# The token of the dot products kept in PSUM instead of SBUF, in a two-layer decoder step with expert retrieval

## The reference, cut to what matters

```
q = (xb @ w_q)                                  # queries, per head 2 halves of 128
s = einsum('bhcd,hcnd->bhcn', q, sk)            # scores against 2 x 128 keys
sv, si = lax.top_k(s, 16) ...                   # two top-16, their 256 sums, top-16 of these
hpre = einsum('bd,bhkd->bhk', xb, u_tab[eid])   # dot products of the token with 128 rows of u
a = gelu(hpre) * softmax(fv)
out = einsum('bhk,bhkd->bd', a, v_tab[eid])     # weighted sum of 128 rows of v
```

## Time and profile before

| | us |
|---|---|
| median of three runs (4362.62, 4367.6, 4372.01) | 4367.6 |
| span of the profiled execution, first to last instruction | 4356.4 |
| POOL busy | 2601.7 |
| DVE busy | 2837.7 |
| PE busy | 2784.1 |
| ACT busy | 601.9 |

### The profile page before, as it was taken

How to read it: one execution, slowest core, us unless ns; L and a number is a source line. 1 busy time by engine, 2 the same in 40 slices (tenths; PEclk the granted TensorE clock), 3 DMA queues, 4 the chain that set the end, 5 groups by cost and what they waited for, 6 DMA issues and landing times.

```text
span 4356.4 us, 41077 instructions
## 1 busy us (share of the span) xinstructions
PE 2784.1 (64%) x7573; PEld 1355.0 (31%) x7573; DVE 2837.7 (65%) x6064; ACT 601.9 (14%) x1614; POOL 2601.7 (60%) x2313
## 2 busy tenths in 40 slices
PE   1498366666656656766778863666666566666566
PEld 1354223233322323322344442232232223322222
DVE  7902777777767777766334347767777677677754
ACT  2110111111111111111122111111111111111011
POOL 2000277777777777776600014778777677777774
PEclk9699688888878888888999976888888888888899
DMA  1540399999999999999900134999999899999997
GB/s 44 44 194 26 121 362 372 370 357 370 379 334 354 374 347 351 368 382 409 398 1 0 52 127 159 364 360 352 356 362 373 328 362 368 342 353 365 359 402 299
DMA packets 355457, 1267.52 MB, mean 291 GB/s; under 512 B 39292, under 2 KB 52092, under 8 KB 351868
## 3 DMA queue, kind: packets, MB, share of 16 engines
q0 software_dynamic: 331776, 1208.11, 73.9%
q1 hardware_dynamic: 23508, 57.71, 4.7%
HBM read 1261.31 MB, written 4.82 MB: 291 GB/s over the span
## 4 chain that ended last, share of the span: by engine, by line
PE 33%; DVE 19%; issue 19%; DMA 14%; POOL 9%; ACT 3%; DVEq 1%; SPq 1%; POOLq 0%; ACTq 0%
PE ps L1370 20%; DMA arena<-in_peer_v,idxv 7%; DMA arena<-in_peer_u,idxu 5%; POOL arena L1577 5%; POOL arena L1565 4%; PE ps L1318 3%; DVE arena L723 2%; DVE arena L712 2%; DVE arena L424 2%; PE ps L1444 2%; PE ps L1459 2%; ACT arena L1064 1%; DVE arena L657 1%; DVE picked L660 1%; PE ps L1340 1%
## 5 line engine op out<-in xcount | busy, mean ns | idle before, releaser
L1370 PE MATMUL ps<-arena 128*128 128x512 f32 x3584 | 1900.8, 679 | 1175.1 <-ACT arena L1064 811.4
L1565 POOL DMA_INDIRECT arena<-in_peer_u,idxu x1152 | 1261.1, 1095 | 1141.8 <-issue 736.0
L712 DVE CUSTOM_DVE_ANT_0 arena<-arena 128x1024 bf16<-128x1024 f32 x1152 | 1387.8, 1226 | 630.6 <-DMA arena<-in_peer_u,idxu 545.7
L1577 POOL DMA_INDIRECT arena<-in_peer_v,idxv x1152 | 1304.7, 1133 | 451.8 <-issue 312.5
L1370 PEld LDWEIGHTS ps<-arena 128*128 128x128 f32 x3584 | 733.4, 216 | 2239.7 <-issue 2114.3
L1064 ACT ACTIVATE arena<-ident,av 128x128 f32<-128x128 f32 x768 | 259.5, 394 | 673.4 <-DVE av L706 423.4
L723 DVE SCALAR_TENSOR_TENSOR arena<-arena,av 128x1024 f32 (+1 forms) x256 | 328.4, 1283 | 6.7 <-DMA arena<-in_peer_v,idxv 6.3
L1340 PE MATMUL ps<-arena 128*128 (+1 forms) x1280 | 300.2, 389 | 10.0 <-DMA arena<-in_peer_wq 5.2
L1340 PEld LDWEIGHTS ps<-arena 128*128 128x128 f32 x1280 | 248.2, 196 | 69.9 <-issue 29.3
L622 DVE MAX8 top<-arena 128x8 f32<-128x128 f32 x128 | 37.0, 289 | 175.0 <-ACT arena L1043 174.7
L1318 PE MATMUL ps<-arena 128*128 128x512 f32 (+1 forms) x320 | 139.7, 599 | 4.4 <-DMA arena<-in_w_glu 4.4
(11 more groups left out here) (214 smaller groups left out, 1966.2 us busy)
## 6 DMA issues: line engine op xcount, KB each, us to landing
arena<-in_peer_u,idxu POOLq DMA_INDIRECT x1152, 6.3
arena<-in_peer_v,idxv POOLq DMA_INDIRECT x1152, 6.3
arena<-in_peer_wq SPq DMA_DIRECT2D x4, 4096.0 KB, 19.8
arena<-in_w_glu SPq DMA_DIRECT2D x2, 4096.0 KB, 13.3
arena<-kern SPq DMA_DIRECT2D x8, 512.0 KB, 22.0
arena<-in_w_q SPq DMA_DIRECT2D x1, 4096.0 KB, 22.9
arena<-in_w_o SPq DMA_DIRECT2D x1, 4096.0 KB, 41.8
arena<-in_gains SPq DMA_DIRECT2D x6, 512.0 KB, 17.5
```

The lines of the kernel that those rows point to most:

```text
L712: dve.tensor_tensor_reduce(JUNK[:, k % 2, :], UROWS[:, k % NU_RING, :], XCUR, 1.0, 0.0, ALU.mult, ALU.add, hp[:, par, k:k + 1]).then_inc(S ...
L1370: mm = pe.matmul(ps[:, half, :], DIAG[:, i % 4, :], VROWS[k % NV_RING][:, half * 512:(half + 1) * 512], start=(starts and i == 0), stop=Fa ...
L1565: pool.indirect_dma_start(UROWS[:, k % NU_RING, :], None, tab_u, bass.IndirectOffsetOnAxis(ap=idxu[:, par, k:k + 1], axis=0))\
L1577: pool.indirect_dma_start(VROWS[k % NV_RING], None, tab_v, bass.IndirectOffsetOnAxis(ap=idxv[:, par, k:k + 1], axis=0))\
```

## The change

The area `XCUR` in SBUF goes; the token is kept in banks 6 and 7 of PSUM. The copy at a tile's first head writes there, and all 16 dots of a slot read it from there. For this, the queries of both parities share bank 4 (columns 0 to 255 and 256 to 511), and the turned queries and the scores of both parities share bank 5: for each parity, the scores are written over the turned queries of the same head.

```diff
-        XCUR = area(20480, D)
...
+        XCUR = ps[:, 6:8, :].rearrange("p a b -> p (a b)")
+        QP = ps[:, 4, :].rearrange("p (a n) -> p a n", a=2)
+        QTP = ps[:, 5, :].rearrange("p (a n) -> p a n", a=2)
...
-                    act.copy(QN[:, par, :], ps[:, 4 + par, 0:2 * P]).then_inc(S["q_copied"], 1)
+                    act.copy(QN[:, par, :], QP[:, par, :]).then_inc(S["q_copied"], 1)
...
-                    act.copy(QT[:, par].rearrange("p a n -> p (a n)"), ps[:, 6 + par, 0:2 * P]).then_inc(S["qt_copied"], 1)
+                    act.copy(QT[:, par].rearrange("p a n -> p (a n)"), QTP[:, par, :]).then_inc(S["qt_copied"], 1)
...
-                    act.copy(SC[:, par].rearrange("p a n -> p (a n)"), ps[:, 6 + par, 256:512]).then_inc(S["sc_copied"], 1)
+                    act.copy(SC[:, par].rearrange("p a n -> p (a n)"), QTP[:, par, :]).then_inc(S["sc_copied"], 1)
...
-                        mm = pe.matmul(ps[:, 4 + par, 0:2 * P], XT[:, k, :],
+                        mm = pe.matmul(QP[:, par, :], XT[:, k, :],
...
-                        mm = pe.transpose(ps[:, 6 + par, i * P:(i + 1) * P], QN[:, par, i * P:(i + 1) * P], ident[:, :])
+                        mm = pe.transpose(QTP[:, par, i * P:(i + 1) * P], QN[:, par, i * P:(i + 1) * P], ident[:, :])
...
-                        mm = pe.matmul(ps[:, 6 + par, 256 + i * P:256 + (i + 1) * P], QT[:, par, i, :],
+                        mm = pe.matmul(QTP[:, par, i * P:(i + 1) * P], QT[:, par, i, :],
```

## The result

The changed kernel takes 4291.35 us (median of 4 runs, 4289.13 to 4293.61), the kernel before 4367.06 in runs beside it: a ratio of 0.9826, with a 95% interval of 0.9812 to 0.984, so 76 us less. The forecast was 4129, 238 us less, with 4055 to 4250. The direction was right, the size was three times too large, and the time lies 41 us above the range.

A forecast was written before the change was run, and what follows sets the result against it. The prediction took POOL to set the pace, its gathers held by DVE's dots. From 4367.6 us, 270 us of released gathers less 16, 10 and 5 left 239 us less: 4129 us, range 4055 to 4250.

The forecast's parts named there:

- That two inputs in SBUF hold a gather and one in PSUM does not: POOL's gathers beside DVE's dots: of 404.6 us above the median gather length (the excess), 270 us goes.
- the short operations: DVE's two 0.69 us operations at and after line 657, 64 times in the slots: they still hold gathers, 17 us.
- The dot's own duration: 1152 dots on DVE: reading the token from PSUM costs 0 us more each.
- the copy of the token into PSUM: DVE's token copy, 10 times: 1.22 us instead of 0.694, so 5 us of the gain is lost.
- The shared banks: PE's queries, turned queries and scores in banks 4 and 5: no added wait in 80 heads, 0 us.
- the rival in which DVE gets slower: The custom dot reads its inputs in turn and takes 2.3 us: at least +236, 4604 us; chance 0.04.
- the one in which the dot still holds POOL: The custom dot holds gathers whatever its inputs are: no gain, 4368 + 5 us; chance 0.05.
- POOL sets the pace before: Both retrievals, 3459 us: POOL's gathers 2565.8, issue 691 and about 200 us of waits set the rows' pace.
- What is late next: Per slot after the change: POOL needs 41.6 us, DVE (33.3 busy) and PE (29.5) stay below that.
- The terms for what doesn't shorten the span: Gain lost at layer starts (16 us), at first heads (10 us) and to the token copy (5 us).
- DMA: Rival in the retrievals: DMA is the bound, ending at 360 GB/s (4368 us) or 380 (4207); chance 0.08.
- The rival with DVE and the rings taking half of the gain: DVE's back-to-back work sets the slot and, with the rings of 8 rows, takes half: 4248 us; chance 0.05.

The follow-up runs named there:

- both moves: Weights made ahead of a slot's first two dots, searches and merge later in DVE's program: 4430.2 us on the kernel before, 4186.8 us on the changed kernel.
- the later searches: Changed kernel with the two top-16 searches and the merge two, two and one dots later in DVE's program: 4179.7 us.
- the versions at 4180: Changed kernel with searches and merge later (4179.7 us), with weights sooner as well (4186.8), or the latter with the merge one dot sooner (4179.1).
- early weights: Kernel before, with the last slot's weights made ahead of the first two dots instead of behind them: 4400.5 us.

## Why the prediction was wrong, point by point

- **That two inputs in SBUF hold a gather and one in PSUM does not: right**, on a custom instruction too. Some 750 gathers inside dots, none held. Of the excess 276 us went, where 270 were forecast, and 129 stayed, where 135 were. That this came so near is in part luck, as two terms missed to opposite sides: 99 us lie on gathers that start inside row adds (115 forecast, 0.39 us for each row add in place of 0.45) and 31 us on those that start inside the short operations (17 forecast).
- **The dot's own duration: right** (1.218 us, forecast 1.22), and so the copy of the token into PSUM (1.228 us, forecast 1.22). **The shared banks: right**, 0 us, by their own run. With them the rival in which DVE gets slower is out, and so is the one in which the dot still holds POOL.
- **POOL sets the pace before: right as far as it went**: with both moves on the kernel before, its excess grew by 97 us and the span by 84, though the wait for the scores had gone. But it set the pace by a narrow margin, as the next point shows.
- **What is late next: wrong, and this is the step that failed.** The prediction set POOL's 41.6 us per slot beside DVE's 33.3 and PE's 29.5 busy us and found room. Busy times summed per engine do not show a chain that crosses engines, in which each waits for another: in the stretch shown, 2.8 us from the slot's start (3754.59) to the weights (3757.40), 17.0 us over ACT, PE and ACT, and 23.8 us of DVE behind the scores (to 3798.23) make 43.6 us, with every engine idle for a part of it. And the 45.8 us per slot that the forecast started from is a mean over a tile, with two long slots in it: the median slot of heads 2 to 7 was 44.7 and 44.0 us already. So the chain left them about 1 us and less, and the forecast asked for 3.7 us less per slot (270/72). The row that pointed to it was in the trace before, the second longest wait of DVE:

```profile
DVE top L622 <- ACT arena L1043: 174.7, 53, 9.0
```

It was not read, because DVE was not the engine that set the pace; but it is a wait of 3.3 us in 53 of the 56 slots that route and are no first head, and rows that come sooner make it longer in place of the slot shorter.
- **The terms for what doesn't shorten the span**: 16 + 10 + 5 = 31 us were forecast, 212.5 us of new idle time came. The two waits of POOL named there, for dots and for products, are the right ones; they were taken as a matter of the first heads alone, but waits of over 4 us for products before a `v` gather, as the one at 3763.18, came 24 times, where there were nine before. The 11.2 us that the forecast kept around the span are no fixed cost either: in the changed kernel the profiled execution took 4289.23 us with a span of 4287.3, 1.9 us less. The forecast compared a median with the span of another execution; the 239 us less do not hang on it.
- **DMA: right, it was not the bound** of the changed kernel. With the later searches single slices reach 408 GB/s, above both ends that the rival had set, and taking a quarter of the bytes away brought 31 us in the changed kernel.
- **The rival with DVE and the rings taking half of the gain** (4248, chance 0.05) was nearest in time, and had the wrong mechanism: not DVE's own gaps, but its wait in order for PE. It was the case with too little chance.

What stays open: what bounds the versions at 4180. With the later searches, POOL's gathers and issue are 2993 us (2302 and 2304 x 0.30), and 1002 us of its idle time holds 691 us of issue, some 145 at the starts and about 165 of other waits; fewer bytes were worth 46 us with both moves, and halving PE's products was not tried on them.

## What to carry to other kernels

When the engine that sets the pace gets faster, compare its new pace with the longest chain through the loop body, not with the other engines' busy times: follow one slot from the first instruction that releases another engine to the one that takes the answer back. And compare with the common slot, not with a mean that takes in a few long ones. A wait that is short but comes in every slot can mark such a chain, and an in-order engine should make early what others wait for and take late what it waits for. The same edit was worth 76 us or some 240 depending on that order, so an edit and the order around it are best measured together.

## What the runs showed of the hardware

A gather held by DVE is held to a point some 0.13 us ahead of the end of the instruction that holds it, then takes its full 0.94 us. Two dots in a row take 2.29 us from start to start of the next pair, 1.15 us each. A gather held by one ends 0.94 us behind that point, the next is issued 0.30 us later, and that is just inside the next dot; so only every second dot lets one through, one per 2.30 us in place of 1.24. That makes the loss a matter of phase: moving one instruction of 0.17 us (early weights) in the kernel before went with 56 us more excess, with dots and row adds as long as before.

The start is not sharp: 29 gathers of the kernel before start within 0.06 us of the start of a row add, and none is held. And one input in SBUF is not always enough to let go: the copy of the token from SBUF to SBUF (L752, 0.69 us) held all five gathers that started inside it, to 1.17 to 1.44 us; inside the copy into PSUM (1.228 us) two started, and both took 0.93 us.

The granted clock of PE enters the chain. Behind 11.42 us in which PE waited for the diagonals, its first three rows took 8.04 us at 3758.66, and the next three 5.39 us at 3767.98. The window over the first ones, and the changed kernel over both (us, PE, PEld, DVE, ACT and POOL busy, PEclk, DMA share, GB/s):

```profile
3759.00:3767.00 8.00, 7.91 (x14) 3.09 (x13) 6.76 (x12) 0.00 (x0) 2.82 (x4) 0.69 0.46 136
3768.00:3773.00 5.00, 5.00 (x12) 2.33 (x13) 0.00 (x0) 0.31 (x2) 3.75 (x4) 1.00 0.91 306
```

The mean granted clock was 0.69 of full speed in the first of them, between the levels of 1.2 and 2.4 GHz (0.5 and 1). In the second it was 1.00, the upper level, and the same work took 2.65 us less. The Trainium skill (TensorE: Matmul & The Clock Gate, Part 1: The HAM clock gate) has the clock fall when PE is idle. The trace agrees: the lower mean stands behind 11.42 us of idle time, and the 1.00 behind 8.04 us of work.
